# Moving the attention-bias gather two feed-forward chunks later, in a two-layer encoder on one core

## The chip, the core and the metric

The kernel runs on one core of one Trainium2 chip. The metric is the device time of one execution in microseconds (us). Five engines work side by side, each through its own list of instructions in order: TensorE (PE, matrix products and transposes), ScalarE (ACT), VectorE (DVE), GpSimd (POOL) and SyncE (SP), which here does nothing but issue weight loads. They wait for each other on counting semaphores. Transfers are made by 16 DMA engines; SP, ACT and POOL issue them.

## The reference

Two layers over 256 tokens of 1024 channels. Each layer adds half a gated feed-forward block, then a mixing block, then half a second feed-forward block:

```python
for l in range(DEPTH):
    x = x + 0.5 * swiglu(rms_norm(x, ffn1_norm[l]), ffn1_w_gate[l], ffn1_w_up[l], ffn1_w_down[l])
    h = rms_norm(x, mix_norm[l])
    z = h @ w_in[l]                       # q, k, v of 8 heads, and p of 4 pooling groups
    a = neighborhood_attention(q, k, v, rpb[l])
    m = multiscale_pool(p, w_pool[l], pool_scale[l])
    x = x + jnp.concatenate([a, m], axis=-1) @ w_out[l]
    x = x + 0.5 * swiglu(rms_norm(x, ffn2_norm[l]), ffn2_w_gate[l], ffn2_w_up[l], ffn2_w_down[l])
return rms_norm(x, final_norm)
```

The attention scores get a learned bias that depends on the row and column distance of query and key. Its table `rpb[l]` has 15 x 31 numbers for each of 8 heads; the kernel spreads it out so that each of 128 partitions (query positions) has its own 6 x 64 numbers for each head.

## The kernel before

**Feed-forward.** The 2816 hidden channels are taken in 11 chunks of 256 (`N_FF_CHUNKS`, numbers 0 to 10; `LAST` is 10). A chunk needs three units of weights of 1 MB each: gate/up rows 0 to 511 (called g0), gate/up rows 512 to 1023 (g1) and the down rows (down). A unit is loaded by SP as two transfers of 512 KB into one of three slots of `w_raw`; ACT splits it into a rounded part `w_hi` (line 472 for g0 and g1, line 465 for down) and DVE into the rest `w_lo` (lines 727 and 718), and PE makes three products of the parts (lines 984, 985, 987). SP issues a slot's next unit when DVE is done with the one before.

**The order in time.** PE's `chunk(i)` does gate/up of chunk i for both token tiles, transposes the gated values of chunk i-1 between the two (line 1081), and then the down products of chunk i-1. Between them ACT stores the transposed values as `gt_hi` (line 529) and DVE the rest as `gt_lo` (line 781); the down products wait for `gt_lo`. ACT and DVE work in a fixed order: split of down(i-1), store of gt(i-1), silu or gate, split of g0(i+1), silu or gate, split of g1(i+1). So what is late for the first of these holds all that stands behind it. The semaphore `g0_used` goes up by one in each chunk, when PE has read the g0 unit for both token tiles.

**The end of a stage.** In the last chunk ACT and DVE split the first unit of the next stage (`mix_unit(layer, 0)`, called mix 0, the parameter `following`) between the two last stores of `gt` (lines 534 and 788). In layer 0, ACT also issues the loads of the pooling matrix, the mask and the last norm's gains there.

**The bias.** Only POOL is concerned. `gather_rows` reads the table of a layer from DRAM and writes it spread out to a DRAM scratch, two transfers of 96 KB for each head (line 385), made of runs of 64 numbers; before each head it waits for a value of `g0_used`, one head in each chunk. For layer 0 that is in the first feed-forward stage of layer 0, for layer 1 in the second feed-forward stage of layer 0. `load_bias` (line 393) waits for all gathers and a later chunk, and loads the spread-out table (1.5 MB) to `bias`. In the mixing block DVE waits for it, applies the mask (line 868) and then adds it to the scores. POOL's list of instructions is: `rstd_of(0)`, gathers of layer 0, load of the table, `rstd_of(1)`, `rstd_of(2)`, gathers of layer 1, `rstd_of(3)`, load of the table, and the other norms' `rstd_of`.

Of the kernel before, what the change touches and what calls it, by code (L numbers as in the profile page):

```python
# [28 lines left out]
N_HEADS = 8  # L29
# [21 lines left out]
DELTAS = ROWS + 2  # L51
STAGES = 3
WARM_UP = 8
PAGE_PAD = 480


# [32 lines left out]
def trunk(nc, x, ffn1_norm, ffn1_w_gate, ffn1_w_up, ffn1_w_down, mix_norm, w_in, rpb, w_pool,  # L89
# [8 lines left out]
    with ctx:  # L98
        def sb(name, shape, dt=F32):
            return ctx.enter_context(nc.sbuf_tensor(name, shape, dt))  # L100

        def sem(name):
            return ctx.enter_context(nc.semaphore(name))


        sb("page_pad", [P, PAGE_PAD])
        w_raw = [sb(f"w_raw{s}", [P, UNIT]) for s in range(SLOTS)]
# [58 lines left out]
        g0_used = sem("g0_used")  # L166
# [72 lines left out]
        def chunk_no(layer, ff, i):  # L239

            return layer * (2 * N_FF_CHUNKS) + ((ff["stage"] // 2) * N_FF_CHUNKS + i)
# [107 lines left out]
        @block.gpsimd  # L349
        def _(pool):  # L350
            nc.gpsimd.memset(minus_half[:, :], -0.5)
            nc.gpsimd.memset(rstd_factors[:, 0:1], 0.5)
            nc.gpsimd.memset(rstd_factors[:, 1:2], HEAD_DIM ** -0.5)
            nc.gpsimd.memset(eps[:, :], RMS_EPS).then_inc(eps_ready, 1)

            def rstd_of(number):
                for t in range(TT):

                    pool.wait_ge(sq_ready[t], number + 1)
                    nc.gpsimd.tensor_tensor(mean_eps[:, t:t + 1], mean_sq[:, t:t + 1],  # L360
                                            eps[:, :], ALU.add).then_inc(mean_ready, 1)
                    pool.wait_ge(mean_ready, number * TT + (t + 1))
                    nc.gpsimd.tensor_tensor(rstd[:, t, :], mean_eps[:, t:t + 1],
                                            minus_half[:, :], ALU.pow).then_inc(rstd_ready[t], 1)
                    pool.wait_ge(rstd_ready[t], number + 1)
                    nc.gpsimd.tensor_tensor(rstd_scaled[:, t, :],
                                            rstd[:, t, :].to_broadcast([P, 2]),
                                            rstd_factors[:, :], ALU.mult
                                            ).then_inc(scaled_ready[t], 1)


            rpb_row = 2 * WIN_COLS - 1
            rpb_head = (2 * WIN_ROWS - 1) * rpb_row
            scratch = bias_dram.rearrange("l p (h e) -> l p h e", h=N_HEADS)

            def gather_rows(layer, ff, number):

                for i in range(N_HEADS):
                    pool.wait_ge(g0_used, chunk_no(layer, ff, i) + 1)
                    for rq in range(P // GRID_W):  # L380
                        first = ((number * N_HEADS + i) * rpb_head
                                 + (WIN_ROWS - 3 - rq) * rpb_row + WIN_COLS - 1)
                        src = bass.AP(rpb.tensor, first,
                                      [[rpb_row, DELTAS], [-1, GRID_W], [1, GRID_W]])
                        pool.dma_start(  # L385
                            scratch[number, rq * GRID_W:(rq + 1) * GRID_W, i, :]
                            .rearrange("p (d c) -> d p c", d=DELTAS), src
                        ).then_inc(bias_rows_loaded, 16)

            def load_bias(layer, after):  # L390
                pool.wait_ge(g0_used, chunk_no(layer, FF1, after) + 1)
                pool.wait_ge(bias_rows_loaded, 16 * 2 * N_HEADS * (layer + 1))
                pool.dma_start(bias[:, :, :, :].rearrange("p h d c -> p (h d c)"),
                               bias_dram[layer, :, :]).then_inc(bias_loaded, 16)

            pool.wait_ge(eps_ready, 1)
            rstd_of(0)
            gather_rows(0, FF1, 0)
            load_bias(0, N_HEADS)
            rstd_of(1)  # L400
            rstd_of(2)
            gather_rows(0, FF2, 1)
            rstd_of(3)
            load_bias(1, 5)
            rstd_of(4)
            rstd_of(5)
            last = STAGES * DEPTH
            pool.wait_ge(sq_ready[0], last + 1)
            nc.gpsimd.tensor_tensor(mean_eps[:, 0:1], mean_sq[:, 0:1], eps[:, :], ALU.add
                                    ).then_inc(mean_ready, 1)  # L410
            pool.wait_ge(mean_ready, last * TT + 1)
            nc.gpsimd.tensor_tensor(rstd[:, 0, :], mean_eps[:, 0:1], minus_half[:, :], ALU.pow
                                    ).then_inc(rstd_ready[0], 1)
            pool.wait_ge(tail_mean_ready, 1)
            nc.gpsimd.tensor_tensor(rstd[:, 1, :], mean_eps[:, 1:2], minus_half[:, :], ALU.pow
                                    ).then_inc(rstd_ready[1], 1)
# [563 lines left out]
        def _(pe):  # L980
# [349 lines left out]
            pe.wait_ge(zeros_ready, 1)  # L1330
            for n in range(WARM_UP):
                last = nc.tensor.matmul(ps[:, n % 2, :], zeros[:, 0:P], zeros[:, :],
# [58 lines left out]
```

## Time and profile before

| | |
|---|---|
| median of 3 runs | 950.64 us (949.08 to 951.82) |
| profiled execution, its own time | 950.42 us |
| its span from first to last instruction | 948.3 us |
| PE busy | 930.1 us (98%) |
| DVE, ACT, POOL busy | 551.7, 499.3, 44.1 us |
| moved by DMA | 174.66 MB, 184 GB/s on average |
| gathers | 32 of 96 KB, median 8.1 us from issue to landing |
| loads of the table | 2 of 1536 KB, median 7.0 us |

The times are those of one execution under the profiler unless a median is named. The 2.1 us between the profiled execution's time and its span lie outside the first and last instruction. Matrix products overlap, so a PE that reads busy may still be short of its best; what tells is where it is idle, and how long a chunk takes.

### The profile page before, as it was taken

How to read it: one execution, taken by the hardware profiler on the slowest of the kernel's cores; microseconds unless marked ns; L12 is line 12 of the kernel's file. 1: busy time of each engine (PE TensorE's matmuls, PEld its weight loads, DVE VectorE, ACT ScalarE, POOL GpSimd, SP SyncE). 2: the span in 40 equal slices, each digit the busy share in tenths (PEclk: the TensorE clock that was granted, in tenths of full speed). 3: DMA queues.
4: the chain of work that ended last, by engine and by line, in shares of the span. 5: the costliest groups of instructions: out<-in, count | busy, mean ns of one | idle time of the engine just before them, and what ended most of it. 6: DMA issues, size and time to landing. Idle time of an engine off the chain costs nothing.

```text
span 948.3 us, 12733 instructions
## 1 busy us (share of the span) xinstructions
PE 930.1 (98%) x4299; PEld 760.0 (80%) x4299; DVE 551.7 (58%) x896; ACT 499.3 (53%) x821; POOL 44.1 (5%) x81
## 2 busy tenths in 40 slices
PE   8899999999999999999999999999999999999996
PEld 6688888887778888888888888888877888888885
DVE  4556455467755655655475545564787474554644
ACT  5545455456746554545475445453675374554542
POOL 1001010010001100100010000000100000000000
PEclk9999999999999999999999999999999999999998
DMA  7976868726235978675356657645534276465541
GB/s 238 244 209 157 224 191 275 264 99 218 104 123 144 272 182 233 161 217 188 133 186 213 221 179 243 213 157 173 173 142 143 77 242 210 168 210 188 168 142 45
DMA packets 123532, 174.66 MB, mean 184 GB/s; under 512 B 8384, under 2 KB 99696, under 8 KB 123248
## 3 DMA queue, kind: packets, MB, share of 16 engines
q1 hardware_dynamic: 117744, 165.70, 52.3%
q0 software_dynamic: 2848, 6.38, 5.7%
q10 hardware_dynamic: 2912, 2.22, 0.7%
q8 instruction: 17, 0.28, 0.1%
q14 instruction: 11, 0.09, 0.0%
HBM read 173.14 MB, written 4.19 MB: 187 GB/s over the span
## 4 chain that ended last, share of the span: by engine, by line
PE 72%; DVE 2%; ACT 1%; issue 1%; DMA 1%; SPq 0%; POOL 0%; POOLq 0%; DVEq 0%
PE ps L984 22%; PE ps L987 22%; PE ps L985 22%; PE ps L1081 1%; DVE w_lo L727 1%; PE ps L1195 1%; PE ps L1211 1%; PE ps L995 1%; PE ps L994 1%; PE ps L1223 1%; DMA w_raw<-in_w_in_dram 1%; PE ps L1069 1%; DVE w_lo L718 0%; PE ps L1044 0%; DVE xt_lo L741 0%
## 5 line engine op out<-in xcount | busy, mean ns | idle before, releaser
L984 PE MATMUL ps<-w_hi,xt_hi 128*128 128x512 f32 x856 | 342.3, 400 | 2.8 <-DVE w_lo L727 1.3
L985 PE MATMUL ps<-w_lo,xt_hi 128*128 128x512 f32 x856 | 334.3, 391 | 0.0
L727 DVE SCALAR_TENSOR_TENSOR w_lo<-w_raw,gains,w_hi 128x512 fp32r<-128x512 f32 x416 | 284.9, 747 | 77.8 <-ACT w_hi L472 76.4
L987 PE MATMUL ps<-w_hi,xt_lo 128*128 128x512 f32 x856 | 329.5, 391 | 0.0
L472 ACT ACTIVATE w_hi<-w_raw,gains 128x512 fp32r<-128x512 f32 x408 | 260.6, 714 | 70.4 <-PE ps L987 65.3
L718 DVE TENSOR_TENSOR w_lo<-w_raw,w_hi 128x1024 fp32r<-128x1024 f32 x104 | 122.8, 1223 | 137.4 <-ACT w_hi L465 137.1
L984 PEld LDWEIGHTS ps<-w_hi,xt_hi 128*128 128x128 f32 x856 | 161.1, 188 | 41.1 <-issue 4.0
L987 PEld LDWEIGHTS ps<-w_hi,xt_lo 128*128 128x128 f32 x856 | 161.1, 188 | 34.8
L985 PEld LDWEIGHTS ps<-w_lo,xt_hi 128*128 128x128 f32 x856 | 161.4, 189 | 30.7
L465 ACT ACTIVATE w_hi<-w_raw 128x1024 fp32r<-128x1024 f32 x104 | 104.4, 1051 | 122.8 <-PE ps L987 113.5
L984 PE MATMUL ps<-w_hi,gt_hi 128*128 128x512 f32 x352 | 138.8, 394 | 4.0 <-DVE gt_lo L781 4.0
L985 PE MATMUL ps<-w_lo,gt_hi 128*128 128x512 f32 x352 | 137.7, 391 | 0.0
L987 PE MATMUL ps<-w_hi,gt_lo 128*128 128x512 f32 x352 | 109.5, 391 | 0.0
L529 ACT ACTIVATE gt_hi<-ps 128x512 fp32r<-128x512 f32 x40 | 23.9, 598 | 138.9 <-PE ps L1081 138.9
L781 DVE TENSOR_TENSOR gt_lo<-ps,gt_hi 128x512 fp32r<-128x512 f32 x40 | 27.7, 692 | 104.4 <-ACT gt_hi L529 104.4
L984 PEld LDWEIGHTS ps<-w_hi,gt_hi 128*128 128x128 f32 x352 | 66.5, 189 | 17.9 <-DVE gt_lo L781 4.4
L987 PEld LDWEIGHTS ps<-w_hi,gt_lo 128*128 128x128 f32 x352 | 66.4, 189 | 14.0
L985 PEld LDWEIGHTS ps<-w_lo,gt_hi 128*128 128x128 f32 x352 | 66.5, 189 | 13.5
L775 DVE SCALAR_TENSOR_TENSOR gated<-ps,rstd_scaled,silu 128x256 f32<-128x256 f32 x88 | 42.0, 478 | 11.0 <-ACT silu L540 11.0
L540 ACT ACTIVATE silu<-ps,rstd 128x256 f32<-128x256 f32 x88 | 41.5, 472 | 8.8 <-PE ps L987 4.2
L385 POOL DMA_DIRECT2D bias_scratch<-in_rpb_dram x32 | 26.4, 828 | 217.7 <-PE ps L987 209.7
L487 ACT ACTIVATE xt_hi<-ps 128x512 fp32r<-128x512 f32 x24 | 13.1, 595 | 40.4 <-PE ps L1069 40.4
(84 smaller groups left out, 405.6 us busy)
## 6 DMA issues: line engine op xcount, KB each, us to landing
w_raw<-in_ffn_w_down_dram SPq DMA_DIRECT2D x88, 512.0 KB, 4.3
w_raw<-in_ffn_w_gate_dram SPq DMA_DIRECT2D x86, 512.0 KB, 4.1
w_raw<-in_ffn_w_up_dram SPq DMA_DIRECT2D x86, 512.0 KB, 5.2
w_raw<-in_w_in_dram SPq DMA_DIRECT2D x32, 512.0 KB, 5.0
w_raw<-in_w_out_dram SPq DMA_DIRECT2D x16, 512.0 KB, 5.2
bias_scratch<-in_rpb_dram POOLq DMA_DIRECT2D x32, 96.0 KB, 8.1
bias<-bias_scratch POOLq DMA_DIRECT2D x2, 1536.0 KB, 7.0
pool_m<-in_pool_matrix_dram ACTq DMA_DIRECT2D x1, 1024.0 KB, 9.0
```

What stands on the lines that cost most here:

```text
L385: pool.dma_start(scratch[number, rq * GRID_W:(rq + 1) * GRID_W, i, :] .rearrange("p (d c) -> d p c", d=DELTAS), src).then_inc(bias_rows_lo ...
L465: nc.scalar.activation(w_hi[slot][:, part], w_raw[slot][:, part], ACT.Copy).then_inc(hi_ready[slot], 2)
L472: nc.scalar.activation(w_hi[slot][:, part], w_raw[slot][:, part], ACT.Copy, scale=g).then_inc(hi_ready[slot], 1)
L529: nc.scalar.activation(gt_hi[:, 0, :, :, :], ps[:, 6, :], ACT.Copy).then_inc(gt_hi_ready, 1)
L540: nc.scalar.activation(silu[:, t, :], ps[:, t, 0:FC], ACT.Silu, scale=rstd[:, t, :]).then_inc(silu_ready[t], 1)
L718: nc.vector.tensor_tensor(w_lo[slot][:, part], w_raw[slot][:, part], w_hi[slot][:, part].bitcast(F32), ALU.subtract).then_inc(lo_ready[slo ...
L727: nc.vector.scalar_tensor_tensor(w_lo[slot][:, part], w_raw[slot][:, part], g, w_hi[slot][:, part].bitcast(F32), ALU.mult, ALU.subtract).t ...
L775: nc.vector.scalar_tensor_tensor(gated[:, t, :], ps[:, t, FC:2 * FC], rstd_scaled[:, t, 0:1], silu[:, t, :], ALU.mult, ALU.mult).then_inc( ...
L781: nc.vector.tensor_tensor(gt_lo[:, 0, :, :, :].rearrange("p k t q -> p (k t q)"), ps[:, 6, :], gt_hi[:, 0, :, :, :].rearrange("p k t q -> ...
L984: nc.tensor.matmul(o, hi, wh, start=start, stop=False)
L985: nc.tensor.matmul(o, hi, wl, start=False, stop=False)
L987: last = nc.tensor.matmul(o, lo, wh, start=False, stop=bool(stop))
```

## The change

A constant of 2 is added to the number of the chunk that each gather waits for, and to that of the first table load. Head i of a layer is gathered after the g0 unit of chunk i+2 is used, not of chunk i: in chunks 2 to 9 of both stages in which gathers are made. The table of layer 0 is loaded at chunk 10, not 8. That of layer 1 keeps its place, chunk 5 of the next layer's first feed-forward stage.

```diff
+GATHER_FROM = 2
...
                 for i in range(N_HEADS):
-                    pool.wait_ge(g0_used, chunk_no(layer, ff, i) + 1)
+                    pool.wait_ge(g0_used, chunk_no(layer, ff, i + GATHER_FROM) + 1)
...
-            load_bias(0, N_HEADS)
+            load_bias(0, N_HEADS + GATHER_FROM)
```

No instruction is added or taken away, and each engine's own list keeps its order; only the semaphore values that POOL waits for differ. All line numbers from here on are those of the kernel before.

## Rows read from the trace of the kernel before

**Rows 1.** The page: span, and busy time by engine.
```profile
span 948.3 us, 12733 instructions
...
PE 930.1 (98%) x4299; PEld 760.0 (80%) x4299; DVE 551.7 (58%) x896; ACT 499.3 (53%) x821; POOL 44.1 (5%) x81
```

**Rows 2.** Waits of PE, whole execution: us in total, times, longest.
```profile
PE ps L984 <- DVE gt_lo L781: 4.0, 1, 4.0
PE ps L1248 <- DVE z L859: 2.3, 2, 1.1
```

**Rows 3.** Timeline of PE: start, us, instruction, [idle before, releaser].
```profile
33.96 0.39 PE L987 MATMUL ps<-w_hi,xt_lo 128*128 128x512 f32 x1
38.34 0.56 PE L984 MATMUL ps<-w_hi,gt_hi 128*128 128x512 f32 x1 [3.98 <-DVE gt_lo L781]
```

**Rows 4.** Timeline of DVE and ACT, 23 to 38 us.
```profile
37.60 0.68 DVE L781 TENSOR_TENSOR gt_lo<-ps,gt_hi 128x512 fp32r<-128x512 f32 x1
```
```profile
23.78 2.57 ACT L472 ACTIVATE w_hi<-w_raw,gains 128x512 fp32r<-128x512 f32 x4 [0.27 <-DMA w_raw<-in_ffn_w_up_dram]
34.16 2.00 ACT L465 ACTIVATE w_hi<-w_raw 128x1024 fp32r<-128x1024 f32 x2 [7.81 <-issue]
36.07 0.58 ACT L529 ACTIVATE gt_hi<-ps 128x512 fp32r<-128x512 f32 x1
```

**Rows 5.** DMA issues, 19.4 to 21 us: count, KB, us from issue to landing.
```profile
w_raw<-in_ffn_w_down_dram SPq DMA_DIRECT2D x1, 512.0 KB, 5.6
...
w_raw<-in_ffn_w_down_dram SPq DMA_DIRECT2D x1, 512.0 KB, 14.1
bias_scratch<-in_rpb_dram POOLq DMA_DIRECT2D x2, 96.0 KB, 11.3
```

**Rows 6.** Timeline of SP: issue of the second half of down 0.
```profile
20.00 0.43 SPq L278 DMA_DIRECT2D w_raw<-in_ffn_w_down_dram  x1
```

**Rows 7.** Windows: engines' busy us, PEclk, DMA share, GB/s.
```profile
22.00:23.00 1.00, 1.00 (x6) 0.84 (x5) 1.00 (x3) 1.00 (x2) 0.00 (x0) 1.00 1.11 399
...
26.00:27.00 1.00, 1.00 (x6) 0.84 (x5) 1.00 (x2) 0.35 (x1) 0.00 (x0) 1.00 1.41 108
...
39.00:40.00 1.00, 1.00 (x4) 0.72 (x4) 1.00 (x3) 1.00 (x3) 0.00 (x0) 0.50 1.21 130
```

**Rows 8.** Timeline of POOL: gathers of layer 0, and the first of layer 1.
```profile
19.77 1.84 POOL L385 DMA_DIRECT2D bias_scratch<-in_rpb_dram  x2
31.93 1.64 POOL L385 DMA_DIRECT2D bias_scratch<-in_rpb_dram  x2 [10.32 <-PE ps L987]
54.60 1.64 POOL L385 DMA_DIRECT2D bias_scratch<-in_rpb_dram  x2 [21.03 <-PE ps L987]
...
138.63 0.83 POOL L385 DMA_DIRECT2D bias_scratch<-in_rpb_dram  x1 [15.17 <-PE ps L987]
143.49 0.83 POOL L385 DMA_DIRECT2D bias_scratch<-in_rpb_dram  x1 [4.04 <-issue]
...
301.81 1.69 POOL L385 DMA_DIRECT2D bias_scratch<-in_rpb_dram  x2 [1.40 <-PE ps L987]
```

**Rows 9.** The page: loads of up, whole execution, and POOL's DMA queue.
```profile
q0 software_dynamic: 2848, 6.38, 5.7%
...
w_raw<-in_ffn_w_up_dram SPq DMA_DIRECT2D x86, 512.0 KB, 5.2
```

**Rows 10.** DMA issues at 145.60 us, and down's pair at 49.5 us.
```profile
w_raw<-in_ffn_w_up_dram SPq DMA_DIRECT2D x1, 512.0 KB, 9.0
```
```profile
w_raw<-in_ffn_w_down_dram SPq DMA_DIRECT2D x2, 512.0 KB, 3.5
```

**Rows 11.** Timeline of ACT, layer 1's gathers just begun.
```profile
315.15 2.56 ACT L472 ACTIVATE w_hi<-w_raw,gains 128x512 fp32r<-128x512 f32 x4 [3.89 <-DMA w_raw<-in_ffn_w_up_dram]
```

**Rows 12.** DMA issue at 179.03 us: second half of mix 0.
```profile
w_raw<-in_w_in_dram SPq DMA_DIRECT2D x1, 512.0 KB, 10.5
```

**Rows 13.** Timelines of ACT, DVE and PE at the end of layer 0's first stage.
```profile
192.13 2.56 ACT L472 ACTIVATE w_hi<-w_raw,gains 128x512 fp32r<-128x512 f32 x4
```
```profile
193.01 2.73 DVE L727 SCALAR_TENSOR_TENSOR w_lo<-w_raw,gains,w_hi 128x512 fp32r<-128x512 f32 x4
197.82 0.43 DVE L788 TENSOR_TENSOR gt_lo<-ps,gt_hi 128x256 fp32r<-128x256 f32 x1 [2.07 <-ACT gt_hi L534]
198.16 1.28 DVE L736 TENSOR_TENSOR resid<-ps,resid 128x512 f32<-128x512 f32 x2
```
```profile
199.96 1.03 PE L1069 MATMUL ps<-ident,resid 128*128 128x128 f32 x8
```

**Rows 14.** Load of layer 0's table (DMA issues), and its first use (DVE).
```profile
bias<-bias_scratch POOLq DMA_DIRECT2D x1, 1536.0 KB, 7.3
```
```profile
219.92 3.56 DVE L868 TENSOR_TENSOR bias<-bias,mask 128x768 f32<-128x768 f32 x4
```

## The prediction

> **What bounds the kernel now.** I read the page first: PE is busy for 930.1 of 948.3 us [rows 1], so a change can only gain where PE is idle or its clock is low, and costs nothing where it delays work that PE does not wait for. Then PE's own waits: the longest single one, 4.0 us, is for `gt_lo` of DVE, and happens once [rows 2]. The timeline puts it at the start of the first stage: the products of chunk 1 begin their last row at 33.96, and the down products of chunk 0 start only at 38.34, after 3.98 us of idleness [rows 3]. PE's granted clock is 1.00 (2.4 GHz) before it and 0.50 (1.2 GHz) in 39 to 40 us, just after it [rows 7]: the stall costs more than its own length.
>
> The length of a chunk gives the whole price. POOL's gathers are released by `g0_used`, once a chunk: at 31.93 for chunk 1, at 54.60 for chunk 2 and at 138.63 for chunk 7 [rows 8]. Chunks 3 to 7 take (138.63 - 54.60) / 5 = 16.81 us each; from 31.93 to 54.60 it is 22.67 us. The excess is 5.86 us: 3.98 of idleness and 1.88 for products at the lower clock and for starting again.
>
> Next I followed the stall back. `gt_lo` ran at 37.60 behind ACT's `gt_hi` at 36.07, which stands in ACT's order behind the split of down 0, begun at 34.16 after 7.81 us of idleness [rows 4]. The view of waits gives no releaser for that ("issue"), but the landings do: the second half of down 0 was issued at 20.00 [rows 6] and took 14.1 us, so it landed at 34.1. The first half, issued half a microsecond earlier, took 5.6 us. What came between is the first pair of gathers, issued from 19.77 on [rows 8]; they took 11.3 us on average [rows 5]. Meanwhile the DMA engines were full but moved little: 399 GB/s at 22 to 23 us, and 108 GB/s at 26 to 27 us with a share that is even higher [rows 7]. So a weight load is held up by short gather runs on the same engines.
>
> **The change, part by part.** *Chunks 0 and 1 of layer 0's first stage lose their gathers.* Without the pair at 19.77, the price of down 0's second half is not in the trace; the bounds are 3.5 us (a pair of down loads with no gather in flight [rows 10]) and 14.1 us (no help at all). I take 5.6 us, its own first half, the nearest row: same queue, same moment, and the same full engines. It then lands at 25.6. What is late next? ACT is free at 23.78 + 2.57 = 26.35 [rows 4], so it starts the split there and not at 34.16, 7.8 us sooner. From the start of that split to PE's first down product there were 38.34 - 34.16 = 4.18 us, so PE could go on at 30.5; it is busy with chunk 1 until about 34.35 [rows 3]. There are 3.8 us to spare: any landing up to 34.35 - 4.18 = 30.2, 10.2 us after issue, hides fully. The stall goes whole, and with it the lower clock, which the trace shows only behind the idleness. Gain: 5.86 us.
>
> *Can another load take its place?* The g0 and g1 units of chunk 2 wait behind the same gathers, and PE reached them without a wait even so [rows 2]; they now start earlier on emptier engines. Nothing to add.
>
> *Chunks 2 to 7* have a pair of gathers at the same point of the chunk as before, at 16.81 us a chunk, which is PE's own pace with nothing waiting. Cost 0, hidden by PE; the margin is that a chunk's loads are issued a chunk ahead.
>
> *Layer 1's gathers* leave chunks 0 and 1 of the second stage (the first was issued at 301.81 [rows 8]). There ACT waited 3.89 us for an up load [rows 11], but PE did not wait. Gain 0, since the stage's first units were loaded before the mixing block ended.
>
> *Chunks 8 and 9 get pairs of gathers, chunk 10 the table.* The place that has least room is the end of layer 0's first stage. In the time scale of before, chunk 9's gather is released at 138.63 + 2 x 16.81 = 172.25. The first transfer goes at once; the second of the last head was held back 4.04 us at 143.49 [rows 8], by its place in POOL's queue, which stays, so it is issued near 177.1. It then meets the second half of mix 0, issued at 179.03, which took 10.5 us already and landed at 189.5 [rows 12]. ACT begins the split of mix 0 at 192.13, DVE ends its part at 195.74 [rows 13]. Behind that in DVE's order stand the last `gt_lo` (0.43 us) and the residual (line 736, 0.64 us a half), which PE's transposes at 199.96 need [rows 13]. So DVE must be free by about 199.96 - 0.64 - 0.43 - 0.1 = 198.8, 3.1 us later than now, and mix 0 may land until 195.2: **5.7 us of room**. What one gather costs a load beside it: the same second transfer at 143.49 was followed by an up load of 9.0 us [rows 10], against 5.2 at the median [rows 9], so 3.8 us. The other bound is the 8.5 us (14.1 less 5.6) of a load that met two. I take 3.8, because only the held-back transfer meets mix 0: below 5.7, cost 0. Both ends are kept.
>
> *The table.* Released near 189 (chunk 10) it lands some 7.3 us later, at about 196, or past 200 if the engines are full; DVE first uses it at 219.92 [rows 14]. Some 20 us of room, cost 0. `rstd_of(1)` stands behind it on POOL, and POOL only issues it and goes on.
>
> The page DMA: Bandwidth & Descriptors of the Trainium skill, section "Why a DMA increments its semaphore by 16 and not by 1", says that a transfer uses as many engines, up to 16, as divide the slowest dimension of its patterns; the gathers' is 6, so each would sit on six engines and hold up any load that needs all 16. Worked out from the 5.7% of POOL's queue [rows 9] less the two table loads at 399 GB/s, a gather would be 1.4 us of 16 engines, or an estimated 3.8 us on each of six; that agrees with the 3.8 us above and would leave the sum as it is.
>
> **Sum.** 950.42 - 5.86 = 944.56 us against the profiled execution, which stands 0.22 us below the median of 950.64. **Forecast for the median: 944.8 us.** A difference of 0.3%, 2.9 us, is about what a measurement of this kernel can tell from none.
>
> **Rivals.**
> 1. *The start-up queue alone makes down 0 late.* For it: the engines are full from 21 us on, with 399 GB/s of weights [rows 7]. Against it: the half issued 0.5 us sooner took 5.6 us. If the second half takes midway between the deadline and now, 12.2 us, 2.0 us of stall and about 0.9 us of lower clock remain: 947.7. At the upper bound nothing is gained: 950.6.
> 2. *Given back at the end of the stage, by sharing.* Two gathers on mix 0 instead of one: it lands 8.5 us later, 2.8 us past its room, plus up to 1.9 us for the clock: 944.8 + 4.7 = 949.5. For it: the engines are at their limit there, with three table loads and two units of weights. Against it: the first transfer of the pair has some 4 us of emptier queue. The same page, section "Issuing engines are not separate DMA queues", says that transfers issued by SP, ACT and POOL interleave on the same 16 engines; by that rule a gather that is moved takes the same engine time elsewhere, which is this rival's ground.
> 3. *Slower: mix 0 blocks ACT and DVE at the end of the stage.* The same place, and one mechanism: price = (delay of mix 0 - 5.7) + 1.9. It eats the whole gain from a delay of 9.7 us on, and is over 0.3% slower from 12.5 us on; with a delay as long as the longest landing seen, 14.1, it gives 944.8 + 10.3 = 955.1. The largest delay that a gather did to a load is 8.5 us, so it needs worse crowding than any in the trace.
> 4. *The change does not take effect*, since some gather is still issued at the start. Nothing speaks for it: `g0_used` counts one for each chunk, so the first gather cannot leave before chunk 2. 950.6.
>
> **How the numbers follow.** Forecast 0.82; first rival 0.09 (half of it still more than 2.9 us faster); given back 0.05; slower by blocking 0.03; no effect 0.01. Faster by over 0.3% is a time under 947.8: 0.82 + 0.045 and a little of the third line, 0.87. Slower by over 0.3%: 0.03. Within: 0.10. The runs of before lie within -1.6 and +1.2 us of their median, which makes the forecast's own range 943.2 to 946.0. The upper end goes to 947.8, which takes in the first rival as far as its middle; what is left out is the rest of that, the given-back cases and outliers below.
>
> **What would show it.** Right: the wait of PE for `gt_lo` near 34 us is gone and the clock stays at 1.00 there; down 0's second half lands in 4 to 8 us; POOL's gathers of layer 0 start near 48.7 and the first six are 16.8 us apart; the last PE product of layer 0's first stage is some 5.9 us earlier; the mix 0 load takes 11 to 15 us and PE does not wait behind it; the table lands before 200. Wrong: a stall of PE left at 34 us (rival 1), or a new one at the transposes near 194 us of the new time scale, with ACT waiting for mix 0 (rivals 2 and 3).

## The result, and the profile after

The changed kernel takes 943.96 us (median of 4 runs, 943.73 to 944.34), the kernel before 950.27 us beside it (4 runs, 949.08 to 951.82). The ratio is 0.9933, with a 95% interval of 0.9922 to 0.9945. The forecast was 944.8 us, with a range of 943.2 to 947.8. The profiled execution took 944.34 us against 950.42 before: 6.08 us less, where the sum said 5.86. In the changed kernel all lines from `GATHER_FROM` on have numbers one higher: the split of down is line 466, the gather line 386, PE's first product line 985.

The page of the changed kernel, span and busy time by engine, to be held against [rows 1]:

```profile
span 942.4 us, 12733 instructions
...
PE 928.2 (98%) x4299; PEld 758.2 (80%) x4299; DVE 551.7 (59%) x896; ACT 499.4 (53%) x821; POOL 44.1 (5%) x81
```

The span is 5.9 us shorter, with the same instructions and the same busy time of DVE, ACT and POOL. PE is busy for 1.9 us less. Most of that lies in the down products behind the old stall: from the first of them to the first product of chunk 2 it was 7.17 us before (38.34 to 45.51) and is 5.44 us now (34.37 to 39.81), 1.73 us less.

PE's waits over the whole execution (us in total, times, longest), as in [rows 2]:

```profile
PE ps L1249 <- DVE z L860: 2.3, 2, 1.1
PE ps L985 <- DVE w_lo L728: 1.5, 3, 1.0
PE ps L1333 <- DVE zeros L708: 1.5, 1, 1.5
PE ps L985 <- DVE xt_lo L742: 1.1, 1, 1.1
```

The wait of 4.0 us for `gt_lo` is gone, and no wait has come in its place. The same step in PE's timeline (start, us, instruction), as in [rows 3]:

```profile
34.14 0.39 PE L988 MATMUL ps<-w_hi,xt_lo 128*128 128x512 f32 x1
34.37 0.39 PE L985 MATMUL ps<-w_hi,gt_hi 128*128 128x512 f32 x1
```

The down products follow the gate/up products without a gap. The landing of down 0's second half (DMA issues at 20 us; the last number is us from issue to landing), as in [rows 5]:

```profile
w_raw<-in_ffn_w_down_dram SPq DMA_DIRECT2D x1, 512.0 KB, 6.6
```

6.6 us in place of 14.1. ACT's timeline, as in [rows 4]:

```profile
24.00 2.56 ACT L473 ACTIVATE w_hi<-w_raw,gains 128x512 fp32r<-128x512 f32 x4 [0.52 <-DMA w_raw<-in_ffn_w_up_dram]
26.60 2.01 ACT L466 ACTIVATE w_hi<-w_raw 128x1024 fp32r<-128x1024 f32 x2
29.10 0.60 ACT L530 ACTIVATE gt_hi<-ps 128x512 fp32r<-128x512 f32 x1 [0.49 <-PE ps L1082]
```

ACT starts the split of down 0 at 26.60, without a wait, and `gt_hi` waits for PE and no longer for ACT's own list. The windows (engines' busy us, PEclk, DMA share, GB/s), as in [rows 7]:

```profile
26.00:27.00 1.00, 1.00 (x6) 0.73 (x5) 1.00 (x3) 0.96 (x2) 0.00 (x0) 1.00 0.91 283
...
39.00:40.00 1.00, 1.00 (x6) 0.84 (x5) 0.00 (x0) 0.00 (x0) 0.00 (x0) 1.00 1.10 385
```

At 26 us the DMA engines move 283 GB/s and not 108, and at 39 us PE's granted clock is 1.00 and not 0.50. POOL's timeline, as in [rows 8], with the table's load:

```profile
48.93 1.83 POOL L386 DMA_DIRECT2D bias_scratch<-in_rpb_dram  x2 [29.25 <-PE ps L988]
...
132.94 1.64 POOL L386 DMA_DIRECT2D bias_scratch<-in_rpb_dram  x2 [15.17 <-PE ps L988]
...
166.54 0.83 POOL L386 DMA_DIRECT2D bias_scratch<-in_rpb_dram  x1 [15.18 <-PE ps L988]
171.91 0.83 POOL L386 DMA_DIRECT2D bias_scratch<-in_rpb_dram  x1 [4.54 <-issue]
183.36 0.60 POOL L394 DMA_DIRECT2D bias<-bias_scratch  x1 [10.61 <-PE ps L988]
```

Chunk 2 is reached at 48.93 and not at 54.60, which is 5.67 us; at chunk 7 (132.94 against 138.63) it is 5.69. So the gain is made before chunk 2 and carried on unchanged through all chunks with gathers. The last transfer is held back by 4.54 us, as it was before (4.04 us), now in chunk 9.

### The profile page after: what moved, and what is told of

The parts are those of the page before. It is cut to its first block, busy times and chain, and to the rows that moved or that the text cites. A ratio compares the mean times of both kernels' runs of the same rounds, so it can differ in the third digit from the quotient of the medians.

```text
span 942.4 us, 12733 instructions
## 1 busy us (share of the span) xinstructions
PE 928.2 (98%) x4299; PEld 758.2 (80%) x4299; DVE 551.7 (59%) x896; ACT 499.4 (53%) x821; POOL 44.1 (5%) x81
## 4 chain that ended last, share of the span: by engine, by line
PE 94%; DVE 3%; ACT 2%; issue 1%; DMA 1%; POOL 0%; POOLq 0%; SPq 0%; DVEq 0%
PE ps L985 29%; PE ps L988 28%; PE ps L986 28%; PE ps L1082 2%; DVE w_lo L728 1%; PE ps L995 1%; PE ps L996 1%; PE ps L1196 1%; PE ps L1070 1%; PE ps L1212 1%; PE ps L1224 1%; DMA w_raw<-in_ffn_w_up_dram 1%; DVE xt_lo L742 1%; ACT xt_hi L488 0%; PE ps L1045 0%
## 5 line engine op out<-in xcount | busy, mean ns | idle before, releaser
L986 PEld LDWEIGHTS ps<-w_lo,gt_hi 128*128 128x128 f32 x352 | 66.1, 188 | 13.4
L985 PEld LDWEIGHTS ps<-w_hi,gt_hi 128*128 128x128 f32 x352 | 66.1, 188 | 13.4
```

Source lines behind the costliest of these rows:

```text
L985: nc.tensor.matmul(o, hi, wh, start=start, stop=False)
L986: nc.tensor.matmul(o, hi, wl, start=False, stop=False)
```

## The experiments

Twelve kernels ran in four groups (experiments 1 to 4, 5 to 8, 9 and 10, 11 and 12), each beside runs of the kernel before (medians 949.78, 950.75, 949.68 and 949.89 us). All diffs are against the changed kernel.

**1. Shift by 1 in place of 2.**

```diff
-GATHER_FROM = 2
+GATHER_FROM = 1
```

> The shift is 1 in place of 2: gathers in chunks 1 to 8, table at chunk 9. Theory (only the pair in chunk 0 makes the stall, since it meets the load of down 0): PE has no wait for gt_lo near 34 us, the clock stays at 1.00 there, the time is that of the shift by 2, 944.0 us within 1. Rival (the pair in chunk 1, beside the gate/up loads of chunk 2, takes part of it): a wait of PE between 25 and 50 us of 1 us or more, and 945.5 to 948 us.

Measured: 944.09 us, ratio 0.9938 (0.9921 to 0.9954). No wait of PE near 34 us; down 0's second half landed in 6.0 us. So no stall is left when the pairs come one chunk later, and the second chunk of the shift buys nothing. (The shift takes the pair out of chunk 0 and moves the one of chunk 1 too; what that leaves open is said below.)

**2. The shift for layer 0's gathers alone, and 3. for layer 1's alone.**

```diff
-            def gather_rows(layer, ff, number):
+            def gather_rows(layer, ff, number, shift):
...
-                    pool.wait_ge(g0_used, chunk_no(layer, ff, i + GATHER_FROM) + 1)
+                    pool.wait_ge(g0_used, chunk_no(layer, ff, i + shift) + 1)
...
-            gather_rows(0, FF1, 0)
-            load_bias(0, N_HEADS + GATHER_FROM)
+            gather_rows(0, FF1, 0, 2)
+            load_bias(0, N_HEADS + 2)
...
-            gather_rows(0, FF2, 1)
+            gather_rows(0, FF2, 1, 0)
```

Experiment 3 has 0, 0 and 2 in these three places.

> Shift 2 for layer 0's gathers and its table load, 0 for layer 1's gathers. Theory: all of the gain is in layer 0's first stage, 944.0 us within 1. Rival (the gathers of the second stage cost PE time that its waits do not show): over 945 us.

> Shift 2 for layer 1's gathers alone; layer 0's gathers and table as before. Theory: 950.3 us within 1, the wait of 4.0 us for gt_lo near 34 us is there as before. Rival (the second stage brings part of the gain): 947 to 949 us.

Measured: 944.04 us, ratio 0.9935 (0.9918 to 0.9952), for layer 0's alone; 949.81 us, ratio 0.9994 (0.9985 to 1.0004), for layer 1's alone, with a PE wait of 4.1 us for `gt_lo`. The whole gain lies in layer 0's first stage.

**4. The table's load alone, at chunk 10.**

The edit is that of experiments 2 and 3, with 0, 2 and 0 in the three places.

> All gathers as before, only layer 0's table is loaded at chunk 10 and not at chunk 8. Theory: the table has 20 us of room and its load hid before, so 950.3 us within 1 and no new wait of PE or DVE. Rival (1.5 MB beside the first units of the mixing block hold up ACT): a new PE wait between 183 and 215 us, 951.5 us or more.

Measured: 949.62 us, ratio 0.9996 (0.9987 to 1.0006), with the wait for `gt_lo` (3.2 us in the profiled execution) and no new one. The later load costs nothing and brings nothing.

**5. One transfer of the pair back in chunk 0.**

```diff
-                    pool.wait_ge(g0_used, chunk_no(layer, ff, i + GATHER_FROM) + 1)
                     for rq in range(P // GRID_W):
+                        pool.wait_ge(g0_used, chunk_no(layer, ff, i + (0 if (i, rq) == (0, 0) else GATHER_FROM)) + 1)
```

> As changed, but the first transfer of head 0 (one of the pair) is left in chunk 0. Down 0's second half may take 10.2 us before PE waits; it took 14.1 with the pair and 6.6 without. Theory of equal shares (each gather holds a load up by about 3.8 us): it takes 9 to 11 us, PE waits 0 to 0.8 us, 944 to 946 us. Rival (one gather on the same engines is enough for all of the delay): 13 us or more, a wait of 3 us or more, 949 us or more.

Measured: 945.82 us, ratio 0.9951 (0.9935 to 0.9968); the second half of down 0 took 11.4 us, PE waited 1.3 us. One gather holds the load up by 11.4 - 6.6 = 4.8 us, more than the 3.8 us expected. The landing is 0.4 us and the wait 0.5 us over what the theory of equal shares allowed, the time within it; the rival's 13 us and 949 us are not reached.

**6. and 7. The gathers spread over the queries, in chunks 0 to 7 and 2 to 9.**

```diff
-GATHER_FROM = 2
+GATHER_FROM = 0   # 6 alone
...
-                                 + (WIN_ROWS - 3 - rq) * rpb_row + WIN_COLS - 1)
+                                 + (WIN_ROWS - 3 - rq) * rpb_row + WIN_COLS - GRID_W)
...
-                                      [[rpb_row, DELTAS], [-1, GRID_W], [1, GRID_W]])
+                                      [[1, GRID_W], [rpb_row, DELTAS], [1, GRID_W]])
...
-                            .rearrange("p (d c) -> d p c", d=DELTAS), src
+                            .rearrange("p (d c) -> p d c", d=DELTAS), src
```

> Gathers in chunks 0 to 7 as before, but with the 64 queries as the slowest dimension and the 6 distances inside (same runs of 64 numbers, same bytes); queries stand mirrored within a grid row, so the bias is a different one. Theory (a gather sits on few engines, so a load over all engines waits for the fullest ones): spread over all 16, a pair costs some 3 us of each, down 0's second half takes 8 to 10 us, PE does not wait, 944.0 to 945 us with the gathers still in chunk 0. Rival (what holds the load up is the total work of many short runs, however they lie): 12 us or more, the stall of some 4 us stays, 949 us or more.

> The spread gathers of the run above (bias mirrored within a grid row), in chunks 2 to 9. Theory: no stall is left that gathers make, so 944.0 us within 0.7, no better than the change alone. Rival (gathers in flight slow PE's steady chunks in a way that shows in no wait): below 943 us.

Measured: 946.12 us, ratio 0.9957 (0.9941 to 0.9974), with the gathers in chunks 0 to 7; 944.36 us, ratio 0.9937 (0.9921 to 0.9954), in chunks 2 to 9, which is the time of the changed kernel, as the theory said. (Their bias is mirrored within a grid row, so the two tell something of the time only.) With the spread pair in chunk 0 the second half of down 0 took 11.5 us and PE waited 1.5 us. That lies between the two theories: the spread takes away part of the delay, not most of it. POOL's queue on the page of experiment 6 (packets, MB, share of 16 engines) speaks against a simple picture of few full engines; the row of before is in [rows 9]:

```profile
q0 software_dynamic: 1824, 6.29, 9.4%
```

The same data take 9.4% of the engines' time and not 5.7%, and a spread gather lands hardly sooner (median of 32: 7.8 us against 8.1). The rule of the Trainium skill (DMA: Bandwidth & Descriptors, "Why a DMA increments its semaphore by 16 and not by 1") that a slowest dimension of 6 puts a transfer on six engines may hold, but no view here shows the engines one by one, and the estimate drawn from it, that spreading makes a pair harmless, is not what was measured.

**8. and 9. Crowding the end of the stage.** Heads 4 to 7 (experiment 8) or heads 2 to 7 (experiment 9) are all gathered in chunk 9.

```diff
-                    pool.wait_ge(g0_used, chunk_no(layer, ff, i + GATHER_FROM) + 1)
+                    pool.wait_ge(g0_used, chunk_no(layer, ff, i + GATHER_FROM if i < 4 else LAST - 1) + 1)   # 8
+                    pool.wait_ge(g0_used, chunk_no(layer, ff, i + GATHER_FROM if i < 2 else LAST - 1) + 1)   # 9
```

> Heads 0 to 3 in chunks 2 to 5, heads 4 to 7 all in chunk 9 in both stages, table at chunk 10: eight gathers in a row in front of mix 0, to price the crowding that the third rival of the prediction needs. By it, eight gathers at 1.4 us of all engines, or up to 3.8 us on those that they use, bring 11 us or more of work: mix 0's second half lands 10 us or more later than 10.5 us after issue, 5.7 us of room are used up, and PE waits 2 to 8 us near 190 to 200 us: 947 to 953 us. Rival (POOL's queue holds back most of them until mix 0 has landed, or the loads go ahead of them): no PE wait, 944.0 us within 1.

> Heads 0 and 1 in chunks 2 and 3, heads 2 to 7 all in chunk 9, in both stages: four gathers more in front of mix 0 than in the run with eight, where it landed at 189.0 us and PE did not wait. By the third rival's room, mix 0 may land until 195.2 - 5.9 = 189.3 us of the new time scale. Theory: four more gathers at 1.0 to 1.4 us of all engines push it to 193 to 195 us, PE waits 3 to 6 us between 188 and 200 us, and the time is 947 to 952 us. Rival (there is more room than worked out, or POOL's queue holds the last ones back): no wait of PE over 1 us and 944.0 us within 1.

Measured, with eight gathers: 944.29 us, ratio 0.9936 (0.992 to 0.9953). ACT's timeline there:

```profile
189.06 2.56 ACT L473 ACTIVATE w_hi<-w_raw,gains 128x512 fp32r<-128x512 f32 x4 [3.04 <-DMA w_raw<-in_w_in_dram]
```

ACT waits 3.04 us for mix 0, and PE still waits for nothing: the load landed at 189.0, just inside the room, which ends at 189.3. So the theory's 10 us of delay was too much: issued at 173.8, the load took 15.2 us, 4.7 us more than the 10.5 us of before. The outcome is the rival's, though by the theory's own room and not by its reason: POOL's queue held back only the last of the eight transfers, and seven left before the load was issued. With twelve gathers: 950.22 us, ratio 1.0 (0.9988 to 1.0012). ACT's timeline and PE's waits there:

```profile
195.09 2.56 ACT L473 ACTIVATE w_hi<-w_raw,gains 128x512 fp32r<-128x512 f32 x4 [8.91 <-DMA w_raw<-in_w_in_dram]
```

```profile
PE ps L1070 <- DVE resid L737: 5.5, 1, 5.5
```

Windows there, columns as above (PEclk is the third number from the end):

```profile
198.00:199.00 1.00, 0.00 (x0) 0.00 (x0) 1.00 (x3) 0.00 (x0) 0.00 (x0) 0.50 0.13 49
```

Mix 0 lands at 195.0, 5.7 us past the room, and PE waits 5.5 us, at the transposes (line 1070) and for the residual, as the third rival said. The granted clock falls to 0.50, and the whole gain is eaten. The third rival's formula fits: mix 0's second half takes 21.9 us from issue to landing and not 10.5, which is 11.4 us more, and 11.4 - 5.7 + 1.9 = 7.6 us; the profiled execution took 951.76 us, 7.4 us over that of the changed kernel.

**10. Two pairs in chunk 0.**

```diff
-                    pool.wait_ge(g0_used, chunk_no(layer, ff, i + GATHER_FROM) + 1)
+                    pool.wait_ge(g0_used, chunk_no(layer, ff, 0 if i < 2 else i + GATHER_FROM) + 1)
```

> As changed, but heads 0 and 1 (two pairs) are gathered in chunk 0. Down 0's second half took 6.6 us with no gather in chunk 0, 11.4 with one and 14.1 with two. Theory (each further gather adds 2.5 to 4 us): 19 to 22 us with four, a PE wait of 9 to 12 us at 34 us with the lower clock behind it, 955 to 959 us. Rival (what is issued after down 0 hardly delays it, only what is issued beside it): 14 to 16 us and 949 to 952 us.

Measured: 945.58 us, ratio 0.9955 (0.9939 to 0.9972); second half of down 0 in 11.3 us, PE wait 1.2 us. Both statements miss: four gathers delay that load less than two do. The theory that each further gather adds its share falls.

**11. Three gathers in chunk 0, and 12. the pair in the other order.**

```diff
-                    pool.wait_ge(g0_used, chunk_no(layer, ff, i + GATHER_FROM) + 1)
                     for rq in range(P // GRID_W):
+                        pool.wait_ge(g0_used, chunk_no(layer, ff, i + (0 if i == 0 else -1 if (i, rq) == (1, 0) else GATHER_FROM)) + 1)   # 11
```

```diff
-GATHER_FROM = 2
+GATHER_FROM = 0
...
-                    for rq in range(P // GRID_W):
+                    for rq in reversed(range(P // GRID_W)):   # 12
```

> As changed, but three gathers stand in chunk 0: the pair of head 0 and the first of head 1. With 0, 1, 2 and 4 gathers there, down 0's second half took 6.6, 11.4, 14.1 and 11.3 us; and the last gather of each burst took longest (11.4 of one, 13.6 after 8.9 of two, 13.9 after 7.6, 9.3 and 9.6 of four). Theory A (the last gather of a burst has a slow end, and the load is held up by it if it is one of the first two): with a third behind it the second gather lands in 9 to 10 us, down 0's second half takes 10 to 12 us, PE waits under 1.5 us, 944.5 to 946 us. Theory B (the delay goes by count and falls again after two by other causes): 12.5 us or more, a PE wait over 2 us, 947 us or more.

> The kernel before (shift 0), with the two transfers of each head in the other order. If the stall depends on place and number of the gathers (theory), nothing changes: down 0's second half takes 13 to 14.5 us, PE waits 3 to 4.5 us, 948.5 to 951 us. If it depends on which addresses the second of the pair reads and writes (rival): the delay differs by more than 2 us, and the time is under 947 us or over 952 us.

Measured: 946.87 us, ratio 0.9978 (0.9963 to 0.9994), with three; its ten runs fall into six of 945.31 to 946.91 and four of 949.86 to 950.35. 947.02 us, ratio 0.9975 (0.9964 to 0.9986), with the pair swapped. In the profiled executions the second half of down 0 took 13.4 and 12.2 us, and PE waited 3.4 and 2.2 us. Theory A of a slow last gather falls (the second gather landed in 9.7 us, as it said, and the load was late all the same). Theory B named the landing and the wait of that execution, but the median of the runs is 0.1 us under its bound. The swap changed the delay by 1.9 us, less than the rival asked for, and the landing, the wait and the time (947.02 us) lie outside what the theory allowed, the time at the edge of the rival's. So neither statement holds as it stands. By the times the order does count: the swap takes off 2.9 us against the kernel before, and the interval of the ratio stays under 1.

**The experiments together.** The table has the changed kernel and every kernel with gathers in chunk 0. One relation holds in all these profiled executions: PE's wait is the landing of down 0's second half less the 10.2 us that the prediction allowed.

| kernel | gathers in chunk 0 | landing, us | less 10.2 | PE's wait, us | execution, us | PEclk fell behind the wait |
|---|---|---|---|---|---|---|
| changed | 0 | 6.6 | under 0 | 0 | 944.34 | no |
| 10 | 4 | 11.3 | 1.1 | 1.2 | 945.50 | no |
| 5 | 1 | 11.4 | 1.2 | 1.3 | 946.37 | no |
| 6 | 2, spread | 11.5 | 1.3 | 1.5 | 945.89 | no |
| 12 | 2, swapped | 12.2 | 2.0 | 2.2 | 946.38 | no |
| 4 | 2 | 13.2 | 3.0 | 3.2 | 949.46 | to 0.50 |
| 11 | 3 | 13.4 | 3.2 | 3.4 | 950.35 | to 0.50 |
| before | 2 | 14.1 | 3.9 | 4.0 | 950.42 | to 0.50 |
| 3 | 2 | 14.1 | 3.9 | 4.1 | 949.92 | to 0.50 |

Windows of PE after the wait in experiment 12, and in experiment 11, one fence each:

```profile
37.00:38.00 1.00, 1.00 (x6) 0.78 (x5) 1.00 (x2) 1.00 (x3) 0.00 (x0) 1.00 1.63 103
```

```profile
38.00:39.00 1.00, 1.00 (x4) 0.79 (x3) 1.00 (x3) 1.00 (x3) 0.00 (x0) 0.50 0.79 276
```

Behind a wait of 2.2 us PE went on at 1.00, with six products in that microsecond; behind 3.4 us at 0.50, with four. So a stall of 1.2 to 2.2 us costs 1.2 to 2.0 us over the changed kernel, and one of 3.2 to 4.1 us costs 5.1 to 6.1 us (differences to 944.34). Before and experiments 3 and 4 have the same pair in chunk 0, and their landings (14.1, 14.1 and 13.2 us) show how far one kernel's executions lie apart: the 13.4 us with three gathers is not told from them.

## Why the prediction was right

*What bounds the kernel.* Right: one stall at the start of the first stage, made by a late half of down 0. Experiments 1 to 4 take the change apart, and only the two in which layer 0's first pair leaves chunk 0 change the time. One gather back in chunk 0 brings back a wait (experiment 5).

*The price of the stall, 5.86 us.* Right: 5.67 us at chunk 2, 5.69 at chunk 7. The 0.19 us between 5.86 and 5.67 were lost earlier: in the changed kernel two products at 25.13 and 25.57 us start 0.44 us apart and not 0.23, and PE begins the last product ahead of the old stall at 34.14 and not at 33.96. From there to the first product of chunk 2 the difference is 5.88 us (11.55 against 5.67). The span shrank by 5.9 us; the other 0.2 us grows in small steps after layer 0's first stage, shows in no wait, and stays unexplained. It is less than the 0.6 us between the four runs of the changed kernel.

*Down 0's landing without gathers, 5.6 us.* It was 6.6, between the bounds of 3.5 and 14.1. The slack of 3.8 us covered the miss. The deadline of 10.2 us was exact to 0.2 us in the eight executions with a wait.

*The lower clock* was said to show only behind the idleness. That is a misreading. In the profiled execution of before it also shows from 8 to 11 us, where that of the changed kernel has 1.00, as these windows show (before, then changed):

```profile
9.00:10.00 1.00, 1.00 (x4) 0.81 (x3) 0.73 (x2) 0.68 (x1) 0.00 (x0) 0.50 0.92 271
```

```profile
9.00:10.00 1.00, 1.00 (x6) 0.70 (x4) 1.00 (x3) 0.56 (x2) 0.00 (x0) 1.00 0.80 246
```

It does no harm to the account: PE waits for `xt_lo` a little later in both, and goes on at 14.42 and 14.36 us. The clock from 34 us on is as the prediction had it.

*The first rival* (the start-up queue alone) falls with the landing of 6.6 us. Its price also had a wrong step: "about 0.9 us of lower clock" behind a stall of 2.0 us. Behind 2.2 us of waiting the clock did not fall at all.

*Chunks 8 to 10.* The gather beside mix 0 was held to cost 3.8 us; mix 0's second half took 10.6 us against 10.5 us before [rows 12], and not the 11 to 15 us named as a sign of being right. DMA issue at 173.33 us in the changed kernel:

```profile
w_raw<-in_w_in_dram SPq DMA_DIRECT2D x1, 512.0 KB, 10.6
```

So the cost of 0 was right, but the 3.8 us behind it were not: what one gather does to a load is not one price (4.8 us in experiment 5, 0.1 us here). *The second and third rivals* had the right place and price. Experiment 9 shows the mechanism with twelve gathers, where the room of 5.7 us and the wait of 5.5 us fit; with the two of the change it is not reached.

*The table.* Right: it landed 7.0 us after 183.36, at 190.4. DVE used it at 214.23, 23.8 us later, as these rows of the load and of DVE's timeline show:

```profile
bias<-bias_scratch POOLq DMA_DIRECT2D x1, 1536.0 KB, 7.0
```

```profile
214.23 3.56 DVE L869 TENSOR_TENSOR bias<-bias,mask 128x768 f32<-128x768 f32 x4
```

*What stays open.* That gathers issued beside down 0's second half delay it is shown; by what rule is not. By number, 1, 3 and 4 gathers gave 11.4, 13.4 and 11.3 us in one profiled execution each, and 2 gave 13.2 to 14.1 us in three; the median times go the same way (945.82, 946.87 and 945.58 us, and 949.6 to 950.8 us with two as in the kernel before). Their spread and their order change the delay, but give no rule. And no run has the pair in chunk 0 without one in chunk 1. In the kernel before, that second pair is issued at 31.93 [rows 8], while down 0's second half is still on its way; it can be behind the last 2.2 us of the landing at most. From 32 to 34 us POOL's queue takes 0.7% of the engines' time, which speaks against a large part, but does not rule it out.

## What to carry to other kernels

A side transfer that is harmless in a steady stage can cost a stall in the first chunks, where the weights are still fetched with no lead; release such work by a chunk's progress, a chunk or two later. To price the stall, take the lengths of the chunks (22.67 against 16.81 us) and not the wait alone, and work out the last landing that still hides: that deadline held where guesses of a transfer's delay did not. When work is moved, work out the same room at the place it moves to.

## What the runs showed that had not been expected

Four gathers in chunk 0 delay the load less than two (11.3 against 13.2 to 14.1 us). The pair of chunk 1, which the kernel with four lacks, does not explain that alone: when it is issued, the load of before has been on its way for 11.9 us already. And the same bytes spread over a larger slowest dimension take more of the DMA engines' time (9.4% against 5.7%) while holding the load up less (11.5 us).

The granted clock makes the cost of a stall uneven. Behind waits of 1.2 to 2.2 us at the first down products it stayed at 1.00 (2.4 GHz); behind waits of 3.2 to 4.1 us in the same place it was at 0.50 (1.2 GHz) for some microseconds, in experiment 4 only from 1.5 us after PE had gone on. The length of the wait is not all that counts: at the start of the kernel, a wait of 1.06 us before the first products was followed by 0.50 in the kernel before, and one of 1.03 us in the same place by 1.00 in the changed kernel (windows above).

The fall of the clock may be why the ten runs with three gathers lie in two groups 3 us apart. Of the ten, only one, in the upper group, has a trace, but each has its mean granted clock on record: 0.994 in all four of the upper group, 0.996 to 0.999 in the six others. That fits, and it does not show where the clock fell. It fits too that the kernels without a stall agree within 1.1 us (943.50 to 944.62 us with the changed kernel and experiments 1, 2, 7 and 8), while the runs of before lie from 947.50 to 951.91 us: the same pair gave waits of 3.2, 4.0 and 4.1 us in three executions.
